# Moving the 64 sums over ada_w out of the first block, into the feed-forward part and the start of the second block

## The chip, the cores and the metric

One core of one Trainium2 chip runs the whole program. The metric is the device time of one execution in microseconds (us), the median of the runs. Times inside an execution come from one profiled execution, and are counted from the start of its span.

## What is computed

Two transformer blocks run one after the other on 256 tokens of width 1024 (T = 256, D = 1024). The second one is modulated: six vectors of 1024 numbers, computed from a conditioning vector `c` and the matrix `ada_w`, shift, scale and gate it, and two more (from `c_ctx`) shift and scale its context.

```python
def first_block(x, ...):
    proj = rmsnorm(x) @ w_in                  # latents, differential q/k/v, 2048 gate columns
    # latent attention (8 heads) and differential attention (4 heads x 2), causal
    x = x + (g_mla * (o_mla @ w_branch_mla) + g_diff * (o_diff @ w_branch_diff)) @ w_out
    x = x + (silu(hn @ w_ffn_gate) * (hn @ w_ffn_up)) @ w_ffn_down     # hn = rmsnorm(x), hidden width 2816
    return rmsnorm(x, norm_final_g)

def second_block(x, c, ctx, c_ctx, ada_w, ada_b, ...):
    mod_x = silu(c) @ ada_w + ada_b           # ada_w is 1024 x 6144
    mod_c = silu(c_ctx) @ ada_w + ada_b
    sh1, sc1, g1, sh2, sc2, g2 = split(mod_x); csh1, csc1 = first two parts of mod_c
    hx = rmsnorm(x) * (1 + sc1) + sh1; hc = rmsnorm(ctx) * (1 + csc1) + csh1
    zx = hx @ w_in2; zc_kv = hc @ w_in2[:, 1024:]
    # pooling and neighbourhood attention on zx, zc_kv
    x = x + g1 * (mixed @ w_out2)
    h2 = rmsnorm(x) * (1 + sc2) + sh2
    x = x + g2 * peer(h2)                     # 8 heads, 16 experts each out of 16384
    return rmsnorm(x, final_g)
```

## The kernel before

The program is written out by hand for each engine (`tensor_program`, `scalar_program`, `vector_program`, `pool_program`, `sync_program`); each engine runs its own list in the order written, and semaphores tie the lists together. So the order of code in a function is the order on its engine.

**The ring.** All weights come through five slots (`RING_SLOTS`), in the order of `ring_plan`. A block is 512 KB, 128 rows of 1024 words. SP issues its load when the slot is released, that is when TensorE is done with the block five places earlier. ScalarE (ACT) copies it to a rounded high part (`sb_hi`, line 922), and VectorE (DVE, line 1244) or GpSimd (POOL, line 1812) subtracts that from the raw words to give the low part (`sb_lo`). The rule that shares them out is `POOL_SHARE`: in the feed-forward part every second block is POOL's, in the context panels of the second block all of them. TensorE multiplies with the high part first, then with the low part. `hi_until` and `lo_until` run three blocks ahead of the panel that an engine serves (`AHEAD`).

**The stages.** First block: input panels (`lat`, `d`), `uq`, `ukv`, gate panels, causal attention (softmax on DVE and ACT, 32 items, with gate panels between them), branch panels `b_mla`, `b_diff`, and `w_out`. GpSimd also does the rotary embedding (`rope`, lines 1832 to 1838), in small operations. Then the feed-forward part: 11 units `u`, each with a gate panel, an up panel and the rows of `w_down` (`rows_onto`). With unit 8 the context tokens come through a ring slot, and are normalised. The second block starts with the context panels `ctx_in2` 2 and 3, beside which the last norm of the first block ("mid") runs, then the norm "mix", the panels `in2` 1, 2, 3, and the neighbourhood attention with panel `in2` 0 beside it.

**The sums over ada_w.** The vectors are computed transposed: row block m of `ada_w.T` (128 x 1024, 512 KB) times the broadcast row silu(c) or silu(c_ctx), summed along the row, gives eight columns per vector. Each is one operation on DVE (line 1260, output `sb_ada_junk`, the sum goes into a column). There are 48 row blocks, and 64 sums, since the first 16 blocks are needed for c and c_ctx. They are issued by `take_ada(key)`, whose number per place is the table `ADA_POINTS`; `ada_slot` gives each block its buffer, and `ada_loads` the place in the ring's order behind which SP issues its load, where it first waits for the sum that used the buffer before. `mod_columns` adds the bias and, for g1 and g2, makes the diagonal that `gate_row` turns into a row by two matmuls. ACT takes silu of `c_rows` (128 x 2048 words) once, at line 991.

**Around the norm "mix".** DVE's order there is: the scaling of "mid" (line 1580), the copy of the first context panel, low parts, the copy of the second, then `norm_both("mix")` with the sum of squares (line 1285) and the scaled rows (line 1523), on which TensorE's transposes for the norm wait (line 570).

## Time and profile before

| what | value |
|---|---|
| median of 3 runs | 1603.01 us (1602.9 to 1603.34) |
| profiled execution | 1604.01 us, of it 1602.2 us of span |
| mean granted TensorE clock | 0.953 of full |
| busy: PE, PEld, DVE, ACT, POOL | 1429.9, 1287.4, 939.9, 711.7, 564.4 us |
| first block up to w_out | about 0 to 270 us |
| feed-forward part | about 272 to 471 us |
| context panels, norm "mix" | about 471 to 508 us |
| in2 panels, neighbourhood attention | about 508 to 608 us |

A busy share over the whole span says little, since the stages have different limits. The clock is given as a share of full speed; 1.00 is 2.4 GHz, and 0.50 the lower level of 1.2 GHz. An engine's idle time counts only where the next thing that ends last is behind it.

### The profile page before, as it was taken

Reading aid. Unit: us, or ns where it says so; the run is one execution under the profiler, and the core shown is the slowest. Engines: PE = TensorE matmul, PEld = TensorE weight load, DVE = VectorE, ACT = ScalarE, POOL = GpSimd, SP = SyncE. Lnnn points to the kernel's source line nnn. Section 1 sums busy time; section 2 is a strip of 40 time slices with the busy share of each in tenths; the row PEclk is TensorE's granted clock in tenths of the full one; section 3 lists DMA queues with packets and bytes.
Section 4 is the critical chain, followed back from the end, with each engine's and each line's share of the span. In section 5 each row is a group of like instructions: output and inputs, shape, how many; then the busy total and the mean of one; then the engine's idle time right before and its main releaser. Section 6 shows DMA issues by size and latency. Waiting matters only on the chain.

```text
span 1602.2 us, 21914 instructions
## 1 busy us (share of the span) xinstructions
PE 1429.9 (89%) x8932; PEld 1287.4 (80%) x8932; DVE 939.9 (59%) x1493; ACT 711.7 (44%) x991; POOL 564.4 (35%) x314
## 2 busy tenths in 40 slices
PE   6878878999997987977467799999999999999997
PEld 6767767999886766877466688999999999999996
DVE  4786677544455565799788655544444444444444
ACT  4544444544444454432222344544444444444442
POOL 2661012444354103677588721221212222121222
PEclk9999879999999999989788899999999999999999
DMA  8564335777774614534200066666555655555554
GB/s 269 157 187 128 110 116 189 250 234 247 238 242 135 204 59 134 173 95 142 82 1 1 21 201 196 209 190 191 185 188 190 188 186 188 191 185 188 191 187 171
DMA packets 183124, 265.74 MB, mean 166 GB/s; under 512 B 8384, under 2 KB 119744, under 8 KB 182768
## 3 DMA queue, kind: packets, MB, share of 16 engines
q1 hardware_dynamic: 182048, 261.47, 50.8%
q8 instruction: 71, 1.16, 0.3%
q0 software_dynamic: 400, 1.25, 0.3%
q10 hardware_dynamic: 576, 1.63, 0.3%
q14 instruction: 29, 0.24, 0.0%
HBM read 259.85 MB, written 4.46 MB: 165 GB/s over the span
## 4 chain that ended last, share of the span: by engine, by line
PE 70%; DVE 14%; POOL 7%; issue 3%; DMA 3%; ACT 2%; SPq 0%; DVEq 0%; POOLq 0%; ACTq 0%
PE bank L614 21%; PE bank L645 17%; PE bank L619 10%; PE bank L650 8%; POOL sb_hot L1951 5%; PE bank L587 4%; PE bank L591 2%; DVE sb_ada_junk L1260 2%; DMA sb_raw<-w_in 2%; PE bank L890 2%; DVE sb_hot L1761 1%; DVE sb_lo L1244 1%; PE bank L829 1%; PE bank L732 1%; PE bank L848 1%
## 5 line engine op out<-in xcount | busy, mean ns | idle before, releaser
L1812 POOL TENSOR_TENSOR sb_lo<-sb_raw,sb_hi 128x1024 fp32r<-128x1024 f32 (+1 forms) x152 | 373.9, 2467 | 904.3 <-ACT sb_hi L922 904.3
L922 ACT ACTIVATE sb_hi<-sb_raw 128x1024 fp32r<-128x1024 f32 (+2 forms) x427 | 444.5, 1048 | 402.0 <-DMA sb_raw<-peer_v 128.7
L1244 DVE TENSOR_TENSOR sb_lo<-sb_raw,sb_hi 128x1024 fp32r<-128x1024 f32 (+2 forms) x276 | 361.7, 1316 | 412.4 <-ACT sb_hi L922 411.8
L614 PE MATMUL bank<-sb_act_hi,sb_hi 128*128 128x256 f32 x1632 | 410.0, 288 | 5.2 <-ACT sb_hi L922 5.2
L614 PE MATMUL bank<-sb_act_lo,sb_hi 128*128 128x256 f32 x1632 | 407.1, 286 | 0.0
L614 PEld LDWEIGHTS bank<-sb_act_hi,sb_hi 128*128 128x128 f32 x1632 | 318.2, 195 | 9.1 <-issue 4.8
L614 PEld LDWEIGHTS bank<-sb_act_lo,sb_hi 128*128 128x128 f32 x1632 | 318.5, 195 | 2.7 <-issue 0.2
L619 PE MATMUL bank<-sb_act_hi,sb_lo 128*128 128x256 f32 x1632 | 233.0, 286 | 21.0 <-POOL sb_lo L1812 21.0
L645 PE MATMUL bank<-sb_hi,sb_hid_lo 128*128 128x512 f32 x600 | 234.3, 391 | 0.0
L645 PE MATMUL bank<-sb_hi,sb_hid_hi 128*128 128x512 f32 x600 | 234.1, 390 | 0.0
L619 PEld LDWEIGHTS bank<-sb_act_hi,sb_lo 128*128 128x128 f32 x1632 | 213.9, 195 | 22.4 <-POOL sb_lo L1812 22.4
L650 PE MATMUL bank<-sb_lo,sb_hid_hi 128*128 128x512 f32 x600 | 160.4, 389 | 0.0
L650 PEld LDWEIGHTS bank<-sb_lo,sb_hid_hi 128*128 128x128 f32 x600 | 112.6, 188 | 23.4
L645 PEld LDWEIGHTS bank<-sb_hi,sb_hid_lo 128*128 128x128 f32 x600 | 112.9, 188 | 21.8
L645 PEld LDWEIGHTS bank<-sb_hi,sb_hid_hi 128*128 128x128 f32 x600 | 112.9, 188 | 21.4
L890 PE MATMUL bank<-sb_hot 128*128 128x128 f32 x512 | 88.0, 332 | 44.3 <-POOL sb_hot L1951 43.6
L890 PEld LDWEIGHTS bank<-sb_hot 128*128 128x128 f32 x512 | 78.2, 236 | 54.3 <-issue 54.2
L1951 POOL TENSOR_TENSOR sb_hot<-sb_hot,sb_pick_T 128x512 f32<-128x512 f32 x64 | 114.4, 1817 | 20.9 <-DVE sb_hot L1761 20.9
L1761 DVE TENSOR_TENSOR sb_hot<-sb_const,sb_pick_T 128x1024 f32<-128x1024 f32 x64 | 107.8, 1708 | 20.1 <-PE bank L890 19.7
L1260 DVE CUSTOM_DVE_ANT_0 sb_ada_junk<-sb_ada_w,sb_c_rows 128x1024 bf16<-128x1024 f32 x64 | 84.2, 1338 | 2.9 <-ACT sb_c_rows L991 2.9
L962 ACT ACTIVATE sb_G<-bank 128x512 f32<-128x512 f32 x64 | 38.2, 597 | 100.2 <-PE bank L890 100.2
L1536 DVE TENSOR_TENSOR sb_hid_lo<-sb_hid,sb_hid_hi 128x512 fp32r<-128x512 f32 x75 | 51.9, 692 | 52.4 <-ACT sb_hid_hi L1212 44.7
(317 smaller groups left out, 1467.6 us busy)
## 6 DMA issues: line engine op xcount, KB each, us to landing
sb_raw<-peer_uT SPq DMA_DIRECT2D x128, 512.0 KB, 3.7
sb_raw<-peer_v SPq DMA_DIRECT2D x128, 512.0 KB, 3.6
sb_raw<-w_in SPq DMA_DIRECT2D x52, 512.0 KB, 4.4
sb_ada_w<-ada_wT SPq DMA_DIRECT2D x48, 512.0 KB, 5.0
sb_raw<-w_gate SPq DMA_DIRECT2D x22, 512.0 KB, 3.9
sb_raw<-w_up SPq DMA_DIRECT2D x22, 512.0 KB, 4.1
sb_raw<-w_down SPq DMA_DIRECT2D x22, 512.0 KB, 3.9
sb_raw<-w_out SPq DMA_DIRECT2D x16, 512.0 KB, 4.4
```

What stands on the lines that cost most here:

```text
L587: e.matmul(opened[t][:, 0:n], part[:, k0 + k, t * P:(t + 1) * P], hi[:, k, :], start=i == first_i and k == 0 and part is x.hi, stop=False)
L614: e.matmul(bank[:, j * T:(j + 1) * T], hi[:, k, j * P:(j + 1) * P], part[:, k0 + k, :], start=i == first_i and j == 0 and k == 0 and part ...
L619: ins = e.matmul(bank[:, j * T:(j + 1) * T], lo[:, k, j * P:(j + 1) * P], x.hi[:, k0 + k, :], start=False, stop=i == last_i and j == 1 and ...
L645: e.matmul(psum(acc, 2 * half_ + t)[:, :], part[:, k, t * P:(t + 1) * P], hi[:, k, :], start=first and k == 0 and part is hid.hi, stop=False)
L650: ins = e.matmul(psum(acc, 2 * half_ + t)[:, :], hid.hi[:, k, t * P:(t + 1) * P], lo[:, k, :], start=False, stop=last and k == 1)
L890: ins = e.matmul(bank[:, j * P:(j + 1) * P], hot[q % HID_BUFS][:, 1, j, :], hot[q % HID_BUFS][:, 0, j, :], start=True, stop=True)
L922: e.activation(flat_of(i, "hi"), flat_of(i, "raw"), ACT.Copy).then_inc(hi_done[i % R], 1)
L1244: e.tensor_tensor(flat_of(i, "lo"), flat_of(i, "raw"), flat_of(i, "hi").bitcast(F32), ALU.subtract).then_inc(lo_done[i % R], 1)
L1260: e.tensor_tensor_reduce(ada_junk[n % 2], ada_bufs[b], c_rows[:, row], 1.0, 0.0, ALU.mult, ALU.add, mcol[name][:, c:c + 1]).then_inc(*ada_ ...
L1761: e.tensor_tensor(hot[q % HID_BUFS], iota.unsqueeze(1).unsqueeze(1).to_broadcast([P, 2, TG, P]), pT[:, 0:2, toks].unsqueeze(3).to_broadcas ...
L1812: e.tensor_tensor(flat_of(i, "lo"), flat_of(i, "raw"), flat_of(i, "hi").bitcast(F32), ALU.subtract).then_inc(lo_done[i % R], 1)
L1951: e.tensor_tensor(h, h, pT[:, 2, q * TG:(q + 1) * TG].unsqueeze(2).to_broadcast([P, TG, P]), ALU.mult).then_inc(*hot_done.inc(q))
```

## The change

The 40 sums that stood in the first block go. The feed-forward part takes 43 (before 16): one behind each gate panel's low parts, two behind each unit's hidden product, one behind each pair of `w_down` blocks. The second block takes 21 (before 8): four behind each of the two context panels' copies, four behind `in2` 1 and 2, three behind `in2` 3, two behind `in2` 0. The silu of `c_rows` moves on ACT from the front of the first block to behind the norm of the feed-forward part. The columns and rows made of the sums move later too: csh1 and csc1 to unit 8, sh1 and sc1 to unit 9, g1's diagonal to unit 10 and its two matmuls behind `in2` 1, sh2 and sc2 behind `in2` 3. Buffers: four for the first 28 row blocks, then seven.

```diff
-ADA_FIRST_BUFS, ADA_BUFS = 3, 4
+ADA_FFN_BUFS, ADA_BUFS = 4, 7
...
-N_ADA, N_ADA_FIRST = 6 * DC, 3 * DC
+N_ADA, N_ADA_FFN = 6 * DC, 28
...
-ADA_POINTS = ([(("lat", 1), 1), (("d", 0), 1), (("d", 1), 2), (("d", 2), 2)]
...
+ADA_POINTS = ([(("w_gate", 0), 1), (("w_up", 0), 1)] + [p for u in range(1, N_FFN) for p in ((("w_gate", u), 1), (("w_up", u), 2), (("down", u - 1), 1))]
+              + [(("down", N_FFN - 1), 1)]
+              + [(("ctx_in2", j), 4) for j in (2, 3)] + [(("in2", j), 4) for j in (1, 2)] + [(("in2", 3), 3), (("in2", 0), 2)])
...
-                after = 6 + m if m < N_ADA_FIRST else span["w_out", 1][-1] + 6 + 2 * (m - N_ADA_FIRST)
+                after = span["down", N_FFN - 1][-1] + 6 + m - N_ADA_FFN
...
@@ scalar_program
-            act.wait_ge(c_in, 32)
-            e.activation(c_rows, c_rows, ACT.Silu).then_inc(*silu_c.inc())
...
             norm_out("ffn", col("norm_ffn_g", 0, 8))
-            act.wait_ge(*ada_done.at(*ada_last[N_ADA_FIRST - 1]))
+            act.wait_ge(c_in, 32)
+            e.activation(c_rows, c_rows, ACT.Silu).then_inc(*silu_c.inc())
...
@@ vector_program
-            ffn_mods = {0: ("csh1", "csc1"), 1: ("sh1", "sc1"), 2: ("g1",), 10: ("sh2", "sc2")}
+            ffn_mods = {8: ("csh1", "csc1"), 9: ("sh1", "sc1"), 10: ("g1",)}
...
                     hid_left(("ffn", u), i)
+                    take_ada("w_up", u)
+                    for name in ffn_mods.get(u, ()):
+                        mod_columns(name)
...
             ctx_copy(2)
+            take_ada("ctx_in2", 2)
             lo_until(("ctx_in2", 3))
             ctx_copy(3)
+            take_ada("ctx_in2", 3)
             norm_both("mix", xr, [normed.at("mid", 1)], [])
```

Three places show what moves. In the names, `sb_ada_junk` is a sum's throwaway output, the row of `sb_mod` alone is the write of its result, and the number behind a name tells buffers apart.

DVE, before, between the copies of the second `uq` panel and of the second `ukv` panel in the first block:

```order
L1319 COPY sb_qm_89<-bank6 128x384
L1260 ISA sb_ada_junk1_118,sb_mod_128<-sb_ada_w1_111,sb_c_rows_108 128x1024
L1260 ISA sb_mod_128 128x1
L1260 ISA sb_ada_junk0_117,sb_mod_128<-sb_ada_w1_111,sb_c_rows_108 128x1024
L1260 ISA sb_mod_128 128x1
L1319 COPY sb_kv_91<-bank0 128x512
L1260 ISA sb_ada_junk1_118,sb_mod_128<-sb_ada_w2_112,sb_c_rows_108 128x1024
L1260 ISA sb_mod_128 128x1
L1260 ISA sb_ada_junk0_117,sb_mod_128<-sb_ada_w2_112,sb_c_rows_108 128x1024
L1260 ISA sb_mod_128 128x1
L1244 TENSOR_TENSOR sb_lo3_63<-sb_raw3_62,sb_hi3_64 128x1024
L1319 COPY sb_kv_91<-bank2 128x512
```

The same place in the changed program:

```order
L1320 COPY sb_qm_89<-bank6 128x384
L1320 COPY sb_kv_91<-bank0 128x512
L1245 TENSOR_TENSOR sb_lo3_63<-sb_raw3_62,sb_hi3_64 128x1024
L1320 COPY sb_kv_91<-bank2 128x512
L1414 COPY sb_km_90<-sb_kv_91 128x8x64 x2
```

The copies and the low parts follow each other with no sum between them; it is so at all 40 places of the first block.

DVE, changed, from the second context panel's low parts to the sum of squares of the norm "mix" (line 1286):

```order
L1245 TENSOR_TENSOR sb_lo1_55<-sb_raw1_54,sb_hi1_56 128x1024
L1320 COPY sb_zc_134<-bank5 128x512
L1261 ISA sb_ada_junk0_117,sb_mod_128<-sb_ada_w0_110,sb_c_rows_108 128x1024
L1261 ISA sb_mod_128 128x1
L1261 ISA sb_ada_junk1_118,sb_mod_128<-sb_ada_w1_111,sb_c_rows_108 128x1024
L1261 ISA sb_mod_128 128x1
L1261 ISA sb_ada_junk0_117,sb_mod_128<-sb_ada_w2_112,sb_c_rows_108 128x1024
L1261 ISA sb_mod_128 128x1
L1261 ISA sb_ada_junk1_118,sb_mod_128<-sb_ada_w3_113,sb_c_rows_108 128x1024
L1261 ISA sb_mod_128 128x1
L1286 ISA sb_xs_76,sb_stat_71<-sb_xres_73 128x1024
```

Before, the sum of squares stands directly behind the copy of `sb_zc`; now four sums stand between them. Four more stand behind the other copy of `sb_zc`, ahead of three low parts.

SP, changed, its queue of loads across the end of the feed-forward part (`w_in2` blocks are the context panels'):

```order
L1975 DMA sb_raw2_58<-w_in2 128x2x512
L1982 DMA sb_ada_w3_113<-ada_wT 128x1024
L1982 DMA sb_ada_w0_110<-ada_wT 128x1024
L1988 DMA sb_band_135<-band 128x2048
L1990 DMA sb_pool_w_136<-pool_w 128x512
L1975 DMA sb_slot3_61<-norm_final_g 128x1024
L1975 DMA sb_raw4_66<-w_in2 128x2x512
L1982 DMA sb_ada_w1_111<-ada_wT 128x1024
L1975 DMA sb_raw0_50<-w_in2 128x2x512
L1982 DMA sb_ada_w4_114<-ada_wT 128x1024
L1975 DMA sb_raw1_54<-w_in2 128x2x512
```

Before, this piece has no load of `ada_wT` at all: the last of the feed-forward part stands ahead of the last `w_down` block, and the next one comes in the middle of the `in2` panels.

## Rows read from the trace of the kernel before

**Rows 1.** The page: costliest groups, and DMA issues, of the sums.
```profile
L1260 DVE CUSTOM_DVE_ANT_0 sb_ada_junk<-sb_ada_w,sb_c_rows 128x1024 bf16<-128x1024 f32 x64 | 84.2, 1338 | 2.9 <-ACT sb_c_rows L991 2.9
...
sb_ada_w<-ada_wT SPq DMA_DIRECT2D x48, 512.0 KB, 5.0
```

**Rows 2.** Windows by stage: length, busy time of each engine, clock, DMA share, GB/s.
```profile
60.00:120.00 60.00, 48.58 (x298) 43.86 (x297) 51.89 (x67) 25.63 (x37) 39.99 (x42) 0.94 0.64 194
120.00:208.00 88.00, 78.06 (x489) 67.64 (x488) 57.08 (x159) 42.73 (x127) 7.13 (x3) 0.86 0.35 108
208.00:275.00 67.00, 50.26 (x301) 45.40 (x300) 50.17 (x83) 30.53 (x48) 14.11 (x7) 0.90 0.54 181
```

**Rows 3.** Windows of the sums alone: DVE busy, count, clock, DMA share, GB/s.
```profile
36.00:283.00 247.00, 53.16 (x40) 0.90 0.48 151
283.00:480.00 197.00, 19.44 (x16) 0.99 0.74 241
```

**Rows 4.** Waits of PE, 40 to 285 us: in total, times, longest.
```profile
PE bank L614 <- DVE sb_ob_lo L1328: 9.3, 1, 9.3
PE bank L587 <- ACT sb_hi L922: 8.6, 2, 7.0
PE bank L591 <- POOL sb_lo L1812: 6.7, 1, 6.7
PE bank L732 <- DVE sb_prob_T L1319: 6.0, 6, 2.8
...
PE bank L719 <- ACT sb_score_bufs L1037: 3.7, 2, 1.9
PE bank L619 <- POOL sb_lo L1812: 3.2, 1, 3.2
```

**Rows 5.** Timeline of ACT at the silu of c_rows: start, us, instruction.
```profile
41.30 1.28 ACT L991 ACT_TABLE_LOAD   x1
42.59 1.91 ACT L991 ACTIVATE sb_c_rows<-sb_c_rows 128x2048 f32<-128x2048 f32 x1
```

**Rows 6.** Timelines of DVE and POOL in the rotary embedding of qm.
```profile
88.62 1.48 DVE L1260 CUSTOM_DVE_ANT_0 sb_ada_junk<-sb_ada_w,sb_c_rows 128x1024 bf16<-128x1024 f32 x1
...
88.97 1.44 POOL L1833 TENSOR_TENSOR sb_rope_tmp<-sb_qm,sb_rope 128x128 f32<-128x128 f32 x1
90.37 0.46 POOL L1834 TENSOR_TENSOR sb_rope_tmp<-sb_qm,sb_rope 128x128 f32<-128x128 f32 x1
```

**Rows 7.** Windows of line 614 alone, at the b_diff panels: PE, PEld, clock, DMA.
```profile
229.00:234.00 5.00, 3.76 (x16) 3.49 (x16) 0.50 0.01 3
235.00:240.00 5.00, 3.48 (x28) 3.22 (x27) 1.00 0.84 279
```

**Rows 8.** Six units of the feed-forward part: window; DVE's and POOL's low parts.
```profile
301.50:403.40 101.90, 101.90 (x718) 95.48 (x717) 50.18 (x62) 43.41 (x47) 44.22 (x18) 1.00 0.74 237
...
L1244 DVE TENSOR_TENSOR sb_lo<-sb_raw,sb_hi 128x1024 fp32r<-128x1024 f32 x18 | 25.5, 1417 | 48.6 <-ACT sb_hi L922 48.6
...
L1812 POOL TENSOR_TENSOR sb_lo<-sb_raw,sb_hi 128x1024 fp32r<-128x1024 f32 x18 | 44.4, 2469 | 59.0 <-ACT sb_hi L922 59.0
```

**Rows 9.** Timelines at the norm "mix": DVE, then PE.
```profile
496.46 3.93 DVE L1244 TENSOR_TENSOR sb_lo<-sb_raw,sb_hi 128x1024 fp32r<-128x1024 f32 x3 [7.07 <-ACT sb_hi L922]
500.91 1.22 DVE L1285 CUSTOM_DVE_ANT_0 sb_xs<-sb_xres 128x1024 f32<-128x1024 f32 x1
...
504.11 2.15 PE L570 MATMUL bank<-sb_const,sb_xs 128*128 128x128 f32 x9 [5.84 <-DVE sb_xs L1523]
```

**Rows 10.** Chain that ended last, at the context panels: start, us, what.
```profile
471.67 5.97 DMA sb_raw<-w_in
...
478.80 4.78 POOL sb_lo L1812 x2
484.19 4.62 DVE sb_xres L1580 x2
```

**Rows 11.** DMA, 466 to 480 us in 40 slices: rate of the queues.
```profile
GB/s 345 222 64 76 12 187 257 222 281 322 316 380 380 415 392 404 363 410 380 433 392 410 416 386 410 392 299 263 228 146 222 217 193 234 222 252 181 170 252 146
```

More of the change, by code:

```diff
@@ L393, in build @@
         c_in = sem("c_in")
-        ada_in = [sem(f"ada{i}_in") for i in range(ADA_FIRST_BUFS + ADA_BUFS)]
+        ada_in = [sem(f"ada{i}_in") for i in range(ADA_BUFS)]
         early_stored = [sem(f"early{i}_stored") for i in range(3)]
@@ L467, in build @@
                 after = ada_block[ada_last[before]] + 7
+            elif m < N_ADA_FFN:
+                after = span["w_out", 1][-1] + 6 + 2 * m
             else:
-                after = 6 + m if m < N_ADA_FIRST else span["w_out", 1][-1] + 6 + 2 * (m - N_ADA_FIRST)
+                after = span["down", N_FFN - 1][-1] + 6 + m - N_ADA_FFN
             ada_loads.setdefault(after, []).append(m)
@@ L789, in tensor_program @@
                 whole(steps)
+                if j == 1:
+                    gate_row("g1")
                 if j == 2:
@@ L1488, in vector_program @@
                 e.tensor_tensor(merged[:, 2 * j:2 * j + 2, :], by_chunk(psum(("b_mla", j))[:, :]), gates_T[:, 2 * j:2 * j + 2, :], ALU.mult).then_inc(*gives(("b_mla", j)))
-                take_ada("b_mla", j)
             for i0 in (0, 2):
@@ L1509, in vector_program @@
                     e.tensor_tensor(v, psum(("w_out", j), t)[:, :], v, ALU.add).then_inc(*gives(("w_out", j), t))
-                if j == 0:
-                    take_ada("w_out", j)
             def norm_both(stage, src, ready, xs_free):
@@ L1609, in vector_program @@
                     heads_out("q", q_T, 4)
+            for name in ("sh2", "sc2"):
+                mod_columns(name)
             def beside_na():
@@ L1984, in load_until @@
                             sp.wait_ge(*ada_done.at(*ada_last[before]))
-                        elif m >= N_ADA_FIRST:
-                            sp.wait_ge(*full(("w_out", 1), NT - 1))
+                        else:
+                            sp.wait_ge(*(full(("w_out", 1), NT - 1) if m < N_ADA_FFN else full("ffn_acc", 3)))
                         e.dma_start(ada_bufs[slot], a["ada_wT"][m * P:(m + 1) * P, :]).then_inc(ada_in[slot], 16)
```

32 lines of the change are left out of this document (9 added, 23 removed).

## The prediction

> **What bounds the kernel now.** I read the page's groups first, for what the sums cost as work: 64 on DVE, 84 us in all, and 48 loads of 512 KB [rows 1]. Then windows by stage and windows of the sums alone: 40 of the 64 stand before 283 us, in 53 us of DVE time, and 16 in the feed-forward part [rows 3]. Then I asked in each stage what TensorE (PE) waits for, since PE has by far the most work; a microsecond of a sum counts only where PE waits behind it.
>
> In the first block PE does wait. From 60 to 275 us DVE is busy 159 of 215 us, and from 60 to 120 us it is the fullest engine, 51.9 of 60 [rows 2]. Six kinds of wait between 40 and 285 us come to 37.5 us [rows 4]; the norm's own wait before the feed-forward part is left out, since the change doesn't touch it. In the feed-forward part PE is busy 101.9 of 101.9 us over six units, while DVE stood idle 48.6 us waiting for ACT's high parts, and POOL 59.0 [rows 8]. So the sums leave a stage where their engine is late and go mostly to one where it has time. The exception is the norm "mix": there PE waits 5.84 us for DVE [rows 9], and the change puts sums directly in front of it.
>
> **The first block, what is taken away.** Durations are of one execution, whose own time was 1604.0 us, 1.0 above the median; I make the sum on that and take 1.0 off at the end.
>
> *Silu on ACT.* The table load and the silu, 1.28 and 1.91 us [rows 5], are directly in front of the high parts for which PE waits 7.0 us [rows 4]. Gain 3.2 us (bounds 2 and 3.2). At its new place ACT loads the silu table anyway for the first hidden unit, and before it waited at that place for the last of the 40 sums; so I cost it at nothing there, behind the three blocks that PE has ready. If that cover were gone it would be 1.9 us, once.
>
> *POOL's rotary embedding.* An operation of POOL that takes 0.46 us alone takes 1.44 when it starts beside a sum of DVE [rows 6]. I count eleven of the 36 such operations between 68 and 99 us lengthened by a sum (the two kinds that differ are shown), 0.7 to 1.0 us each, about 10 us with one low part of POOL. This chain ends in POOL's low parts, for which PE waits 6.7 and 3.2 us [rows 4]. The first wait closes; of the second about 1.1 us stays, because PE arrives earlier too. Gain 8.8 (bounds 5, if other work of DVE stretches them instead, and 9.9, both waits whole).
>
> A page bears on it. The Trainium skill, "SBUF — State Buffer", says that DVE and GpSimd share one port pair as an exclusive lock, and that a DVE operation with two SBUF inputs and a GpSimd one that reads SBUF cannot run together. The 0.46 against 1.44 us agree with it. By the lock alone the gain here would be the whole blocked time, 11 x 1.0 = 11 us, an estimate from that page; I take the smaller number since only PE's waits can be given back.
>
> *Causal attention.* The waits for `sb_prob_T` and for `sb_score_bufs`, 6.0 and 3.7 us [rows 4], follow on pairs of sums, each about 2.4 us (19.44 / 16 = 1.2 us a sum [rows 3]), that stand ahead of the next scores and copies. Gain 7.5 of 9.7 (bounds 4 and 9.7); the rest is the latency of the softmax chain.
>
> *Branch panels.* PE waits 9.3 us for `sb_ob_lo` [rows 4], and in DVE's order four sums and the four products of b_mla stand ahead of it. Four sums are 4.8 us; one low part that POOL blocked may come free as well. Gain 5.5 (bounds 4.5 and 7.3). The second wait for high parts, 8.6 - 7.0 = 1.6 us [rows 4], is at w_out's last block behind DVE's chain of merges with three sums in it: gain 1.6 (bounds 0 and 1.6).
>
> *The clock.* After the 9.3 us wait the granted clock is 0.50, and 16 matmuls of a panel take 3.76 us where 28 take 3.48 at full clock [rows 7]: 0.235 against 0.124 us each. Over the three stages the clock takes (1 - 0.94) x 60 + (1 - 0.86) x 88 + (1 - 0.90) x 67 = 22.6 us [rows 2], partly idle time. With the waits closed, fewer stretches fall to 0.50. Which ones, no row can say; I take 6 us (bounds 1 and 16).
>
> Sum of gains: 3.2 + 8.8 + 7.5 + 5.5 + 1.6 + 6.0 = 32.6 us.
>
> **The later places, what is added.** *Feed-forward part.* 27 more sums at 1.2 us are 32 us of DVE time in 205. Per unit they add two, 2.4 us, where DVE idles 48.6 / 6 = 8.1 us [rows 8]; cost nothing while that cover holds. The loads stay two a unit up to unit 7, since two sums share a block, and become four from unit 8. At unit 9 the extra sums, sh1 and sc1 stand ahead of the context norm's low parts; ACT waits for those inside its own list, and the high parts queued behind it come 2.4 to 3 us later against a lead of about three blocks. I take 1.0 (bounds 0 and 3). g1's two matmuls only change place, about 1.7 us on PE in both.
>
> *The norm "mix".* DVE's chain there: low parts until 500.3, copy, sum of squares at 500.91, and PE's transposes at 504.11 after 5.84 us of waiting [rows 9]. The first four sums fit into the 7.07 us in which DVE waited for high parts [rows 9]. The second four stand between the copy and the sum of squares: 4 x 1.2 less the overlap of back-to-back sums, 4.6 us, entirely on the path (bounds 4.6 and 7, with one of them blocked by a POOL low part). Queued behind them are the norm, PE's transposes and all `in2` panels.
>
> *Their loads.* Two blocks of `ada_wT` now stand ahead of the band, the gain row and the load issued at 471.67, and one behind it. That load took 5.97 us, and ACT, two POOL low parts and the "mid" scaling hang on it in a row [rows 10]. The queues run at about 400 GB/s between 470 and 475 us [rows 11], so a load of 512 KB takes 1.3 us of them and two take 2.6. I take 2.7, with a little of the third (bounds 0, if the queue has drained, and 5).
>
> *in2 panels and the second attention.* Each of the panels `in2` 1 to 3 is preceded or followed by a burst of up to four loads, and up to three more sums; PE was never idle there, a burst of four takes 4 x 1.3 = 5.2 us of the queues, which is about two blocks of the three that lie ready: 1.0 (bounds 0 and 4). One sum fewer in `in2` 0 (-1.2) and a later start of the attention (+1.5): 0.3.
>
> Sum of costs: 1.0 + 4.6 + 2.7 + 1.0 + 0.3 = 9.6 us. Nothing behind 608 us changes.
>
> 1604.0 - 32.6 + 9.6 = 1581.0, less 1.0 for the median: **1580.0 us**.
>
> **The rivals.** *A, the sum above* (chance 0.63): between 1570 and 1591.
>
> *B, half of the gain is lost in the first block* (0.19): closing one wait uncovers the next, above all the ring's loads, whose slots are released by PE itself, or the softmax chain. For it: the DMA share of 0.64 from 60 to 120 us [rows 2]; against it: the 24 row blocks that the sums load there, 12.6 MB, leave that stage too. Gain 17, costs 9.6: 1603 - 17 + 9.6 = 1595.6; up to 1600.
>
> *C, more* (0.12): the clock stays at its upper level almost through, 16 instead of 6, and the costs at the mix norm stay at the low bound: 1603 - 42.6 + 6.5 = 1567.
>
> *D, slower: DVE and POOL block each other in the feed-forward part* (0.06). Six units take 101.9 us; POOL's low parts take 44.4 and DVE's 25.5 of them [rows 8], twelve sums 14.6 and twelve more as much again: 99 us of work that cannot overlap, if DVE and POOL exclude each other there as in [rows 6]. If low parts come late by 3 us a unit, PE loses 33 us over 11 units: 1603 - 32.6 + 9.6 + 33 = 1613. It decides from about 2.1 us a unit (23 / 11). Against it: low parts run three blocks ahead, and a block of PE takes 101.9 / 36 = 2.8 us, so 8.5 us. A POOL low part of 2.47 us [rows 8] can hold a sum up, and a sum a low part. The Trainium skill, "SBUF — State Buffer", has it so: of two operations that need the shared pair, the second waits for the whole of the first.
>
> **How the numbers follow.** A measurement tells this kernel's change from none at about 0.2%, 3.2 us. Range: A, and somewhat over half of B and of C, 0.81 together: 1568 to 1597. Faster by over 0.2%: A, B and C, 0.94; within 0.2%: 0.02; slower: 0.04; these two are D.
>
> **What would show it.** Right: no sums before 270 us; POOL's rotary operations at 0.3 to 0.5 us; the first block ends about 33 us earlier; PE still full in the feed-forward part; the wait before the mix norm 12 to 14 us instead of 5.84, with four sums in front of the sum of squares. Wrong: waits for low parts of PE in the feed-forward units (D), waits for high parts behind DMA in the first block (B), or a wait at unit 8's context block much over its 2.9 us.

## The result, and the profile after

The changed kernel takes **1582.49 us** (median of 4 runs, 1576.31 to 1585.24) against 1602.97 us (4 runs); the ratio is 0.9866, with a 95% interval of 0.9837 to 0.9896. It is faster by 20.5 us. The forecast was 1580.0 (1568 to 1597).

The profiled execution of it took 1583.26 us, with a span of 1581.4. I laid TensorE's landmarks of both traces side by side: the first transposes of a norm (rows of line 570 before, 572 after), and the first matmul of the first context panel.

| landmark on PE | before | after | lead |
|---|---|---|---|
| end of the attention stage, ahead of the first `b_mla` panel | 215.35 | 190.15 | 25.2 |
| norm ahead of the feed-forward part | 272.00 | 239.87 | 32.1 |
| first context panel | 471.48 | 438.78 | 32.7 |
| norm "mix" | 504.11 | 482.31 | 21.8 |
| norm behind the second attention | 638.07 | 617.95 | 20.1 |
| end of the span | 1602.2 | 1581.4 | 20.8 |

So all of the gain arises before 240 us, the feed-forward part keeps it, and a third of it is lost in one stretch of 44 us, between the first context panel and the norm "mix".

**The first block.** The waits of PE after, 40 to 285 us (in total, times, longest); they answer to [rows 4]:

```profile
PE bank L621 <- POOL sb_lo L1807: 6.1, 1, 6.1
PE bank L572 <- DVE sb_xs L1514: 5.3, 1, 5.3
PE bank L616 <- DVE sb_ob_lo L1329: 3.6, 1, 3.6
PE bank L589 <- ACT sb_hi L924: 3.0, 1, 3.0
PE bank L734 <- DVE sb_prob_T L1320: 2.8, 6, 0.8
PE bank L616 <- ACT sb_hi L924: 0.7, 1, 0.7
PE bank L721 <- ACT sb_score_bufs L1037: 0.2, 1, 0.2
```

The six kinds of [rows 4] were 37.5 us; their successors here (without L572, the norm's own) are 16.4. The wait for POOL's first low part (6.7) is gone, but the second has grown from 3.2 to 6.1. That is 21.1 us of the 32.1 in the table of landmarks; most of the rest is the clock. The whole attention stage, from the end of POOL's second wait to the first `b_mla` panel, in windows (length, PE, PEld, DVE, ACT, POOL busy, clock, DMA share, GB/s), before and then after:

```profile
102.24:215.35 113.11, 101.64 (x680) 90.52 (x680) 78.11 (x203) 58.97 (x157) 14.02 (x7) 0.89 0.37 117
```

```profile
93.39:190.15 96.76, 93.47 (x680) 84.26 (x680) 56.17 (x168) 57.95 (x156) 11.79 (x7) 0.97 0.32 93
```

Both hold the same 680 matmuls. The stage is 16.35 us shorter: 8.2 us less idle time (113.11 - 101.64 against 96.76 - 93.47), and 8.2 us less busy time for the same matmuls. Where the latter comes from is seen in windows of 4 us of PE alone, in the trace of before (length, PE busy, clock, DMA share, GB/s):

```profile
124.00:128.00 4.00, 1.13 (x9) 1.00 0.84 262
128.00:132.00 4.00, 4.00 (x24) 0.57 0.00 0
132.00:136.00 4.00, 3.48 (x27) 1.00 0.51 135
...
164.00:168.00 4.00, 1.97 (x8) 0.72 0.73 262
168.00:172.00 4.00, 4.00 (x21) 0.50 0.00 0
172.00:176.00 4.00, 4.00 (x23) 0.93 0.38 131
```

Up to 127.45 PE waited 2.81 us for `sb_prob_T`, and up to 166.79 it waited 2.03. Behind each wait stands a stretch at or near the lower level, 1.2 GHz, in which PE is full and does 21 to 24 matmuls in 4 us; from 136 to 144 us, at 1.00, it does 35. Two more waits of the stage, of 1.94 us (up to 152.11) and 1.73 us (up to 194.31), are followed by windows at 0.57 and 0.56. So these four waits cost about as much again behind them. After the change the longest wait in the stage is 0.81 us, and from 100 to 190 us the granted clock is 1.00 throughout.

**The sums at their new places** (the page's group, and its DMA issue), against [rows 1]:

```profile
L1261 DVE CUSTOM_DVE_ANT_0 sb_ada_junk<-sb_ada_w,sb_c_rows 128x1024 bf16<-128x1024 f32 x64 | 119.2, 1894 | 1.2 <-DMA sb_ada_w<-ada_wT 1.2
...
sb_ada_w<-ada_wT SPq DMA_DIRECT2D x48, 512.0 KB, 5.9
```

The same 64 sums take 119 us instead of 84. They stand beside POOL's low parts now, and each side holds the other up. This is the window of [rows 8] moved by the lead of 32.1 us, so over the same six units, with POOL's low parts in it:

```profile
269.40:371.30 101.90, 101.90 (x722) 96.15 (x721) 83.16 (x78) 44.83 (x48) 51.70 (x18) 1.00 0.77 249
...
L1807 POOL TENSOR_TENSOR sb_lo<-sb_raw,sb_hi 128x1024 fp32r<-128x1024 f32 x18 | 51.7, 2872 | 51.7 <-ACT sb_hi L924 51.7
```

POOL's low parts rose from 2469 to 2872 ns and DVE's busy time from 50.2 to 83.2 us, and PE is still busy 101.90 of 101.90 us. The whole part took 198.9 us (239.87 to 438.78), before 199.5.

**The stretch that lost.** It is 43.5 us long, before 32.6. DVE's timeline (start, us) at the end of the feed-forward part, where PE's last product ended at 438.95:

```profile
437.55 2.36 DVE L1267 TENSOR_TENSOR sb_stat<-sb_stat,sb_cols 128x8 f32<-128x8 f32 x1
439.94 5.91 DVE L1276 TENSOR_SCALAR sb_gate_diag<-sb_const,sb_stat 128x128 f32<-128x128 f32 x8
445.76 1.22 DVE L1261 CUSTOM_DVE_ANT_0 sb_ada_junk<-sb_ada_w,sb_c_rows 128x1024 bf16<-128x1024 f32 x1
...
446.90 1.22 DVE L1261 CUSTOM_DVE_ANT_0 sb_ada_junk<-sb_ada_w,sb_c_rows 128x1024 bf16<-128x1024 f32 x1
...
448.05 2.48 DVE L1555 TENSOR_TENSOR sb_xres<-bank,sb_xres 128x512 f32<-128x512 f32 x4
```

The four adds of `ffn_acc` onto `sb_xres` (the last row) end 11.6 us after PE's last product; before they ended 0.9 us after it. In front of them stand sums, g1's bias and its diagonal. Those that ran beside POOL's low parts were slowed: a sum at 434.19 took 3.42 us, the bias (128x8) 2.36 us, the eight tiles of the diagonal 5.91 us. POOL was idle from 444.6 to 448.3, and the two sums there took 1.22 us each, as when alone. SP's queue of loads shows a second effect:

```profile
439.46 0.51 SPq L1975 DMA_DIRECT2D sb_raw<-w_in  x1
447.01 0.33 SPq L1982 DMA_DIRECT2D sb_ada_w<-ada_wT  x1
447.38 0.43 SPq L1975 DMA_DIRECT2D sb_raw<-w_in  x1
```

SP stood still for 7 us, because the load of `ada_wT` at 447.01 needs a buffer that the delayed sum at 445.76 was using; the load of `w_in2` queued behind it came as late. It had stood still once before, until 437.65, behind the sum that took 3.42 us, so that the band (1 MB) and the gain row went out just ahead of the `w_in2` load of 439.46. ACT's squares of "mid" stand in its list behind the high parts of those blocks:

```profile
452.89 1.06 ACT L924 ACTIVATE sb_hi<-sb_raw 128x1024 fp32r<-128x1024 f32 x1 [4.64 <-DMA sb_raw<-w_in]
453.85 1.04 ACT L1106 ACTIVATE sb_xs<-sb_xres 128x1024 f32<-128x1024 f32 x1
```

The squares started 14.9 us after PE's last product (before 8.5). They did not wait for the adds, which had ended 3.3 us earlier, but for the high part ahead of them, and this for its load. "mid" scaled its rows 18.1 us after the product (before 12.6). Last, PE at the mix norm, against the row of PE in [rows 9]:

```profile
482.31 3.00 PE L572 MATMUL bank<-sb_const,sb_xs 128*128 128x128 f32 x13 [10.43 <-DVE sb_xs L1514]
```

I split the 10.9 us that the stretch lost at the start of "mid"'s scaling: 5.5 us (18.1 - 12.6) ahead of it, and 5.4 (25.3 - 19.9) behind it, where the second four sums stand. Below, "the product" is PE's last product of the feed-forward part.

### The profile page after: what moved, and what is told of

It reads as the page before. It is cut to its first block, busy times and chain, and to the rows that moved or that the text cites. A ratio compares the mean times of both kernels' runs of the same rounds, so it can differ in the third digit from the quotient of the medians.

```text
span 1581.4 us, 21911 instructions
## 1 busy us (share of the span) xinstructions
PE 1426.2 (90%) x8932; PEld 1284.4 (81%) x8932; DVE 974.3 (62%) x1493; ACT 708.7 (45%) x989; POOL 560.5 (35%) x314
## 4 chain that ended last, share of the span: by engine, by line
PE 53%; DVE 10%; POOL 5%; DMA 1%; issue 1%; ACT 1%; SPq 0%; DVEq 0%; ACTq 0%
PE bank L647 15%; PE bank L616 14%; PE bank L652 7%; PE bank L621 7%; POOL sb_hot L1946 5%; PE bank L589 3%; PE bank L892 2%; DVE sb_hot L1756 2%; PE bank L593 1%; PE bank L831 1%; PE bank L850 1%; DVE sb_i12f L1695 1%; DMA sb_raw<-w_in 1%; DVE sb_pick L1716 1%; DVE sb_eq L1707 1%
## 5 line engine op out<-in xcount | busy, mean ns | idle before, releaser
L1807 POOL TENSOR_TENSOR sb_lo<-sb_raw,sb_hi 128x1024 fp32r<-128x1024 f32 (+1 forms) x152 | 382.8, 2525 | 879.1 <-ACT sb_hi L924 879.0
L621 PE MATMUL bank<-sb_act_hi,sb_lo 128*128 128x256 f32 x1632 | 232.6, 286 | 23.2 <-POOL sb_lo L1807 23.2
L647 PEld LDWEIGHTS bank<-sb_hi,sb_hid_lo 128*128 128x128 f32 x600 | 112.9, 188 | 21.8
L1261 DVE CUSTOM_DVE_ANT_0 sb_ada_junk<-sb_ada_w,sb_c_rows 128x1024 bf16<-128x1024 f32 x64 | 119.2, 1894 | 1.2 <-DMA sb_ada_w<-ada_wT 1.2
```

Of the source, the lines that this page charges most:

```text
L621: ins = e.matmul(bank[:, j * T:(j + 1) * T], lo[:, k, j * P:(j + 1) * P], x.hi[:, k0 + k, :], start=False, stop=i == last_i and j == 1 and ...
L647: e.matmul(psum(acc, 2 * half_ + t)[:, :], part[:, k, t * P:(t + 1) * P], hi[:, k, :], start=first and k == 0 and part is hid.hi, stop=False)
L1261: e.tensor_tensor_reduce(ada_junk[n % 2], ada_bufs[b], c_rows[:, row], 1.0, 0.0, ALU.mult, ALU.add, mcol[name][:, c:c + 1]).then_inc(*ada_ ...
L1807: e.tensor_tensor(flat_of(i, "lo"), flat_of(i, "raw"), flat_of(i, "hi").bitcast(F32), ALU.subtract).then_inc(lo_done[i % R], 1)
```

## The experiments

Each was timed in rounds with the kernel before on the same chip; its median there was 1602.0 to 1604.0 us. "Stretch" is from PE's first context matmul to the mix norm.

### What the sums of the first block cost, each stage by itself

Three kernels are the one before with some sums over 8 words instead of 1024, the place, the load and the silu being kept.

```diff
-                    e.tensor_tensor_reduce(ada_junk[n % 2], ada_bufs[b], c_rows[:, row], 1.0, 0.0, ALU.mult, ALU.add,
+                    wd = 8 if key[0] in ("lat", "d", "uq", "ukv", "gate", "b_mla", "b_diff", "w_out") else D
+                    e.tensor_tensor_reduce(ada_junk[n % 2][:, 0:wd], ada_bufs[b][:, 0:wd], c_rows[:, row][:, 0:wd], 1.0, 0.0, ALU.mult, ALU.add,
```

> The kernel before, with the 40 sums of the first block over 8 words instead of 1024, so that csh1, csc1, sh1, sc1 and g1 are not the reference's; the loads, the silu and all places stay. This is the removal alone, without the later costs. By the prediction's terms it gains 8.8 (rotary embedding) + 7.5 (attention) + 5.5 + 1.6 (branch panels) + 6 (clock) = 29.4 us: 1573.5, and the feed-forward part's norm starts at 242.6 instead of 272.0. Rival (the 24 loads of the first block, 12.6 MB, hold up the ring's loads as well): 24 us or less, 1579 or more. If the changed kernel's 32.1 us there are 3 to 4.4 for the silu, 28 to 29 are left for this kernel and none for the loads.

Measured 1574.58 us (1571.41 to 1576.91), ratio 0.9826 (0.9811 to 0.9842): 28 us. The feed-forward part's norm starts at 244.80, 27.2 us earlier than before, against the 28 to 29 that the changed kernel gained there without the silu. The rival falls: with all 24 loads still there the gain is over its 24 us, and what the loads held up is 1 to 2 us at most.

The second has only the 16 sums beside the attention short:

```diff
+                    wd = 8 if key[0] == "gate" else D
```

> The kernel before, with the 16 sums behind its eight gate panels, that is beside the attention, over 8 words instead of 1024; parts of sh1, sc1 and g1 are not the reference's. From the end of the second wait for POOL's low parts to the first b_mla panel the kernel before takes 113.1 us, the changed one 96.8; the waits for the softmax there sum to 9.1 and 2.3 us, and the clock of 120 to 208 us was 0.86. Theory 1 (the waits pull the clock down, and the clock costs more than they do): the whole 14 to 16 us come back from these 16 sums alone, time 1587 to 1589, clock about 1.00 there. Theory 2 (the clock has another cause, for instance the stage ahead): 7 us, 1596.

Measured 1588.09 us (1583.92 to 1588.29), ratio 0.9897 (0.988 to 0.9913): 16 us, from 16 sums.

```profile
103.28:198.09 94.81, 91.35 (x680) 82.04 (x680) 63.38 (x206) 59.20 (x157) 13.22 (x7) 1.00 0.46 145
```

This is the window of the attention stage again: the same 680 matmuls in 91.35 us, at clock 1.00. The idle time in it fell by 8.0 us (11.5 to 3.5) and the busy time by 10.3. No sum ahead of the stage was changed, so theory 1 stands: with the waits gone, the clock stays up.

The third has only the 14 sums from `lat` to `ukv` short:

```diff
+                    wd = 8 if key[0] in ("lat", "d", "uq", "ukv") else D
```

> The kernel before, with the 14 sums from the latent panel to the second ukv panel over 8 words instead of 1024; parts of csh1, csc1, sh1 and sc1 are not the reference's. The prediction gave 8.8 us to them by POOL's rotary operations. Theory 1 (as predicted): the waits of TensorE for POOL's low parts go from 6.7 and 3.2 to 0 and 1.1, time 1594. Theory 2 (other work of VectorE, low parts and copies, blocks POOL in place of the sums, and TensorE arrives earlier): the first wait goes, the second becomes 5 to 6 us, gain 4 to 5, time 1598 to 1599.

Measured 1596.61 us (1594.57 to 1600.25), ratio 0.9961 (0.9946 to 0.9975): 6 to 7 us. PE's waits for POOL there, in one row where before there were two of 6.7 and 3.2:

```profile
PE bank L619 <- POOL sb_lo L1813: 5.1, 1, 5.1
```

The waits are theory 2's; the time lies between the two. In the trace the feed-forward norm starts 6.0 us earlier, 4.8 of them in these waits. Why the second wait stays is seen in POOL's timeline of the changed kernel, and DVE's beside it:

```profile
82.33 0.47 POOL L1827 TENSOR_TENSOR sb_rope_tmp<-sb_qm,sb_rope 128x128 f32<-128x128 f32 x1 [7.68 <-DVE sb_qm L1320]
...
83.59 1.45 POOL L1830 TENSOR_TENSOR sb_rope_tmp<-sb_qm,sb_rope 128x128 f32<-128x128 f32 x1
...
86.76 1.44 POOL L1828 TENSOR_TENSOR sb_rope_tmp<-sb_qm,sb_rope 128x128 f32<-128x128 f32 x1
88.16 1.52 POOL L1829 TENSOR_TENSOR sb_rope_tmp<-sb_qm,sb_rope 128x128 f32<-128x128 f32 x1
...
91.00 2.34 POOL L1807 TENSOR_TENSOR sb_lo<-sb_raw,sb_hi 128x1024 fp32r<-128x1024 f32 x1
```

```profile
83.39 1.32 DVE L1245 TENSOR_TENSOR sb_lo<-sb_raw,sb_hi 128x1024 fp32r<-128x1024 f32 x1 [0.72 <-ACT sb_hi L924]
...
86.40 1.48 DVE L1245 TENSOR_TENSOR sb_lo<-sb_raw,sb_hi 128x1024 fp32r<-128x1024 f32 x1
88.14 1.23 DVE L1245 TENSOR_TENSOR sb_lo<-sb_raw,sb_hi 128x1024 fp32r<-128x1024 f32 x1 [0.26 <-ACT sb_hi L924]
```

POOL had idled 7.7 us: the chain can't start before DVE has copied `sb_qm` out of the banks. Then three operations of 0.46 us still take 1.45, now beside DVE's own low parts at 83.39, 86.40 and 88.14. So a chain of 8.7 us with a low part of 2.3 behind it stays, and PE waits for its end.

### The silu alone, put back

The changed kernel, with ACT's silu at its old place:

```diff
@@ scalar_program
+            act.wait_ge(c_in, 32)
+            e.activation(c_rows, c_rows, ACT.Silu).then_inc(*silu_c.inc())
             for j, dst in enumerate((dq, dk, dv)):
...
             norm_out("ffn", col("norm_ffn_g", 0, 8))
-            act.wait_ge(c_in, 32)
-            e.activation(c_rows, c_rows, ACT.Silu).then_inc(*silu_c.inc())
```

> The changed kernel, with the silu of c_rows back at its old place on ScalarE, in front of the high parts of the first panels. Theory 1 (the silu and its table load, 1.28 + 1.91 us, were on the path): TensorE's wait at 40 us grows from 2.98 to about 6.2 and the time by 3.2 to 1585.7. Theory 2 (the loads bound that stage, and the silu sat in a wait for them): time stays within 1 us of 1582.5.

Measured 1586.88 us (1583.61 to 1587.44), ratio 0.9903 (0.9885 to 0.9921); PE's wait at 40 us:

```profile
PE bank L589 <- ACT sb_hi L924: 6.0, 1, 6.0
```

It grew from 2.98 to 5.99, 3.0 us, as theory 1 has it. The medians differ by 4.4; the 1.4 more are within the scatter of the runs. The intervals of the two ratios overlap (0.9885 to 0.9921, and 0.9837 to 0.9896), so the wait in the trace decides.

### The four sums ahead of the mix norm

```diff
-            take_ada("ctx_in2", 3)
             norm_both("mix", xr, [normed.at("mid", 1)], [])
             norm_lo("mix")
+            take_ada("ctx_in2", 3)
```

> The changed kernel, with the four sums between the copy of the second context panel and the norm "mix" moved behind that norm's low parts. Theory 1 (the four sums are wholly on the path, as the prediction has it): the wait of TensorE before the mix norm falls from 10.43 us by 4.6 to about 5.8, and the time from 1582.5 to about 1578. Theory 2 (that wait comes from late loads and from the chain ahead of the second context panel, and the sums only fill it): the wait stays over 9 us and the time stays at 1582. Theory 3: the four sums only move, and now hold up the copies and low parts for the panel in2 1; a new wait of 2 to 5 us there, time 1580 to 1583.

Measured 1578.04 us (1574.86 to 1581.31), ratio 0.9852 (0.9832 to 0.9872).

```profile
476.67 1.73 PE L572 MATMUL bank<-sb_const,sb_xs 128*128 128x128 f32 x7 [5.82 <-DVE sb_xs L1514]
```

The wait is 5.82 us, before the change 5.84, and the median is 4.4 us lower: theory 1. The intervals of the ratios overlap (0.9832 to 0.9872, and 0.9837 to 0.9896), so here too the 4.6 us are read from the wait and not from the times. There was no new wait in the panel `in2` 1, so theory 3 falls. The stretch is still 38.8 us against 32.6.

### What makes "mid" late: the diagonal, the loads, or the sums

One kernel moves g1's bias and diagonal behind the mix norm:

```diff
-            ffn_mods = {8: ("csh1", "csc1"), 9: ("sh1", "sc1"), 10: ("g1",)}
+            ffn_mods = {8: ("csh1", "csc1"), 9: ("sh1", "sc1")}
...
             norm_lo("mix")
+            mod_columns("g1")
```

> The changed kernel, with g1's bias and its diagonal of eight tiles moved on VectorE from the end of the feed-forward part (unit 10) to behind the low parts of the norm "mix". In the changed kernel they take 2.36 and 5.91 us from 437.55 us on, and behind them stand two sums, the adds of ffn_acc at 448.05 and the sum for whose end SyncE's queue of loads waits until 447.01. Theory 1 (this lateness is what the end of the feed-forward part lost beyond the forecast): the adds come 6 to 8 us earlier, the w_in2 load issued at 447.38 comes at about 441, the small waits of TensorE in the context panels (6.1 us in all) fall to about 3, and the time is 1578 to 1580. Theory 2 (the amount of the loads there, 512 KB each at 1.3 us of the queues, is what counts): the adds come earlier but TensorE's waits stay, time 1582.

Measured 1582.42 us (1580.44 to 1583.17), ratio 0.9875 (0.9856 to 0.9894): no gain, against theory 1's 3 us. With the diagonal away, the sums behind it run beside POOL's low parts:

```profile
436.26 3.42 DVE L1261 CUSTOM_DVE_ANT_0 sb_ada_junk<-sb_ada_w,sb_c_rows 128x1024 bf16<-128x1024 f32 x1
...
439.62 3.42 DVE L1261 CUSTOM_DVE_ANT_0 sb_ada_junk<-sb_ada_w,sb_c_rows 128x1024 bf16<-128x1024 f32 x1
...
442.96 3.41 DVE L1261 CUSTOM_DVE_ANT_0 sb_ada_junk<-sb_ada_w,sb_c_rows 128x1024 bf16<-128x1024 f32 x1
...
446.30 2.48 DVE L1555 TENSOR_TENSOR sb_xres<-bank,sb_xres 128x512 f32<-128x512 f32 x4
```

The adds still end 7.8 us after PE's last product. SP no longer stood still there (the next `w_in2` load at 443.76, 2.8 us after the product instead of 8.4), but the one before it, issued at 441.57 with the others in flight, was used by ACT only at 450.36, 8.8 us later; in the changed kernel this took 7.7 us, and before the change 6.0. "mid" started 16.1 us after the product. So with the standstill gone the loads in flight took over: the time is theory 2's.

Both moves in one kernel:

> Both of the two moves above, the four sums and g1's diagonal behind the norm "mix". If each is on the path by itself the gains add up to 7 to 9 us: 1574 to 1576. If they share one wait (the norm's start is set by whichever is later) the time is that of the better one, 1578. VectorE then has 4.6 + 5 us of work ahead of the copies of the panel in2 1, and if low parts become late there, up to 5 us come back.

Measured 1576.92 us (1574.52 to 1578.13), ratio 0.9843 (0.9826 to 0.986), 1.1 less than with the four sums alone, which these runs can't tell from nothing; stretch 38.0. ACT's wait for the `w_in2` load that was issued at 438.30, 9.5 us before its use:

```profile
447.84 1.06 ACT L924 ACTIVATE sb_hi<-sb_raw 128x1024 fp32r<-128x1024 f32 x1 [9.27 <-DMA sb_raw<-w_in]
```

SP issued its next `w_in2` load at 440.25, without a standstill, the adds ended 7.8 us after the product, and "mid" started only 17.2 us after it.

The next takes volume off the queues and leaves DVE alone:

```diff
-                        e.dma_start(ada_bufs[slot], a["ada_wT"][m * P:(m + 1) * P, :]).then_inc(ada_in[slot], 16)
+                        wd = 8 if m in (24, 25, 26, 27, 31, 32, 33, 34) else D
+                        e.dma_start(ada_bufs[slot][:, 0:wd], a["ada_wT"][m * P:(m + 1) * P, 0:wd]).then_inc(ada_in[slot], 16)
```

> The changed kernel, with eight of the loads of ada_wT around the end of the feed-forward part (row blocks 24 to 27 and 31 to 34) cut from 1024 to 8 words per row; all sums keep their full length, over what the buffers held, so g1 and parts of sh2 and sc2 are not the reference's. This takes 4 MB off the queues between about 405 and 452 us and nothing off VectorE. Theory 1 (volume: the w_in2 load issued at 439.46 landed 7.7 us later because two loads of ada_wT, the band and the gain row were ahead of it): it lands within 6 us, the stretch from the first context panel to the mix norm shrinks from 43.5 us by 2 to 4, time 1578.5 to 1580.5. Theory 2 (only VectorE's work ahead of the norm counts): stretch and time unchanged, 1582.

Measured 1581.0 us (1576.73 to 1581.92), ratio 0.9863 (0.9845 to 0.9882); stretch 43.0, adds 11.6 us and "mid" 17.5 us after the product. The `w_in2` load issued at 437.07 was used 7.2 us later instead of 7.7, and not within the 6 of theory 1. Taking these eight loads away alone gives 0.6 us of the stretch. But SP still stood still for the sum, until 444.62, so this kernel does not show what the transfers cost once nothing else holds "mid" up.

The opposite leaves the loads and takes DVE's time of the 21 sums of the second block away:

```diff
+                    wd = 8 if key[0] in ("ctx_in2", "in2") else D
```

> The changed kernel, with its 21 sums of the second block over 8 words instead of 1024, so that g2 and parts of sh2 and sc2 are not the reference's; all loads stay. This takes VectorE's time of these sums away and leaves their loads. Theory 1 (the second four sums are the only ones on the path): as the kernel with these four moved, 4.6 us, time 1578; the stretch from the first context panel to the mix norm stays about 6 us longer than before (32.6), from the loads. Theory 2 (the first four, 6.2 us with one lengthened, delay the low parts and the second copy too): stretch within 2 us of before, time 1572 to 1574.

Measured 1577.46 us (1576.91 to 1579.65), ratio 0.985 (0.9836 to 0.9863); stretch 39.6, "mid" 19.0 us after the product and the mix norm 20.5 behind that. Theory 1: beyond the second four, no cost of the second block's sums is seen; what is left is ahead of "mid".

### Versions that take both away

The first attempt was crude: five sums a unit, none beside the context panels.

```diff
-ADA_POINTS = ([(("w_gate", 0), 1), (("w_up", 0), 1)] + [p for u in range(1, N_FFN) for p in ((("w_gate", u), 1), (("w_up", u), 2), (("down", u - 1), 1))]
+ADA_POINTS = ([(("w_gate", 0), 1), (("w_up", 0), 1)] + [p for u in range(1, N_FFN) for p in ((("w_gate", u), 1), (("w_up", u), 2), (("down", u - 1), 2))]
               + [(("down", N_FFN - 1), 1)]
-              + [(("ctx_in2", j), 4) for j in (2, 3)] + [(("in2", j), 4) for j in (1, 2)] + [(("in2", 3), 3), (("in2", 0), 2)])
+              + [(("in2", 1), 4), (("in2", 2), 3), (("in2", 3), 2), (("in2", 0), 2)])
```

> Five sums a unit in the feed-forward part instead of four (two behind each pair of w_down blocks), none beside the context panels, four, three, two and two in the in2 panels; g1's diagonal behind the norm "mix"; the loads for the second block issued some blocks later than in the changed kernel. 53 sums stand in the feed-forward part. If the cover there holds (TensorE still full, 199 to 200 us for the part) and both VectorE's sums and the loads beside the context panels were what the stretch to the mix norm lost, that stretch is back to 33 to 35 us and the time is 1571 to 1574. If only the four sums on the path counted: 1576 to 1578. Against it: 0.9 loads more per unit, and a fifth sum beside POOL's low parts; if low parts come late by 1 us a unit the time is 1582 or more.

Measured 1586.03 us (1585.6 to 1586.4), ratio 0.9899 (0.9884 to 0.9915): slower than the change. The feed-forward part takes 206.0 us instead of 198.9; PE waits twice 0.5 us for DVE's low parts in the middle of it, and between 395 and 431 us 1.6, 4.0 and 1.5 us for high parts (before the change two such waits stood in the part, of 0.9 and 2.9 us; what delays them more here was not taken apart). And four slowed sums now stand ahead of the adds, which end 11.1 us after the product. So at four sums a unit the cover of the feed-forward part holds. At five it starts to give: 1.0 us of waits for low parts is seen, and whether the late high parts belong to it is open.

This kernel also parts the adds from the loads. Its adds end about as late as the changed kernel's, but SP's four `w_in2` loads behind the product have no load of `ada_wT` between them and no standstill. "mid" starts 15.3 us after the product, not 18.1, and here ACT does wait for an add:

```profile
457.16 1.06 ACT L1108 ACTIVATE sb_xs<-sb_xres 128x1024 f32<-128x1024 f32 x1 [1.18 <-DVE sb_xres L1557]
```

The second attempt clears DVE's way to the adds: no sums in unit 10 behind its gate panel, five a unit only up to unit 5, 20 in the second block.

```diff
+ADA_POINTS = ([(("w_gate", 0), 1), (("w_up", 0), 1)] + [p for u in range(1, N_FFN - 1) for p in ((("w_gate", u), 1), (("w_up", u), 2), (("down", u - 1), 2 if u <= 5 else 1))]
+              + [(("w_gate", N_FFN - 1), 1)]
+              + [(("ctx_in2", j), 3) for j in (2, 3)] + [(("in2", j), 4) for j in (1, 2, 3)] + [(("in2", 0), 2)])
...
+            norm_both("mix", xr, [normed.at("mid", 1)], [])
+            norm_lo("mix")
+            mod_columns("g1")
+            take_ada("ctx_in2", 3)
...
+            if m >= N_ADA_FFN:
+                after = max(after, span["down", N_FFN - 1][-1] + 8 + m - N_ADA_FFN)
```

> The changed kernel, with nothing ahead of the adds of ffn_acc on VectorE at the end of the feed-forward part: the four sums of unit 10 behind its gate panel go, five instead of four a unit stand in units 1 to 5, three sums behind the first context copy, three and g1's diagonal behind the norm "mix", four each behind in2 1 to 3, two behind in2 0; loads for the second block later. In the changed kernel the adds end 11.6 us after TensorE's last product of the part, before 0.9; the scaling of "mid" starts 18.1 us after it, before 12.6. Theory 1 (this lateness is 5.5 of the 10.9 us that the stretch to the mix norm lost, and the second four sums the rest): adds end at about 1, "mid" starts at 12.5 to 13.5, the mix norm 33 to 34 us after the last product instead of 43.4, time 1572 to 1574. Theory 2 (the loads of w_in2 themselves are slowed by the other loads in flight): "mid" starts at 15 or later, time 1575 to 1577.

Measured 1576.5 us (1569.71 to 1578.16), ratio 0.9823 (0.9802 to 0.9843). The feed-forward part takes 201.2 us, with two waits of 0.5 us for DVE's low parts again, so the fifth sum isn't quite free in units 1 to 5 either. The adds end 0.9 us after PE's last product and "mid" starts 10.7 us after it, earlier than before the change. So the first 5.5 us came from what this kernel took away there: DVE's late work, SP's standstills behind it, and the loads of `ada_wT` among the `w_in2` loads (none stands between the four of 440.13 to 448.66). It took them away together, so it does not say how much is whose, and it is no test of its theory 2, the loads in flight. With only a part of it taken away "mid" stayed late: 17.5 us after the product with the eight loads cut, 16.1 and 17.2 without the second standstill, and 15.3 in the kernel with five sums a unit, where the adds were late but not the loads. But the norm "mix" came 34.6 us after the product. ACT's timeline behind "mid":

```profile
459.67 1.06 ACT L926 ACTIVATE sb_hi<-sb_raw 128x1024 fp32r<-128x1024 f32 x1 [5.25 <-DMA sb_raw<-w_in]
463.40 1.06 ACT L926 ACTIVATE sb_hi<-sb_raw 128x1024 fp32r<-128x1024 f32 x1 [2.68 <-DMA sb_raw<-w_in]
466.00 1.06 ACT L926 ACTIVATE sb_hi<-sb_raw 128x1024 fp32r<-128x1024 f32 x1 [1.54 <-DMA sb_raw<-w_in]
468.64 1.06 ACT L926 ACTIVATE sb_hi<-sb_raw 128x1024 fp32r<-128x1024 f32 x1 [1.58 <-DMA sb_raw<-w_in]
```

The four blocks come 2.6 us apart and more: a load of `ada_wT` stands in front of each but the first. The last kernel moves these:

```diff
-                after = max(after, span["down", N_FFN - 1][-1] + 8 + m - N_ADA_FFN)
+                after = max(after, span["down", N_FFN - 1][-1] + (8 if m < N_ADA_FFN + 3 else 13 + (m - N_ADA_FFN - 3) // 2))
```

> The kernel adds_first with its loads of ada_wT for the second block moved: three behind the fourth w_in2 load (where the queues have time, before the scaling of "mid" gives the gain row's slot back), the others not before the last w_in2 block of the second context panel. In adds_first the scaling of "mid" started 10.7 us after TensorE's last product (before: 12.6), but the mix norm came 23.9 us after that start (before: 19.9), and ScalarE waited 2.68, 1.54 and 1.58 us for the three w_in2 loads that followed the first one, each with a load of ada_wT in front of it; before 0.83, 0.29, 0.30. Theory 1 (these loads in front are the 4 us): the waits fall to under 1 us each, mix norm 30 to 31.5 us after the last product instead of 34.6, time 1572 to 1573.5. Theory 2 (VectorE's three sums there, two of them lengthened by POOL, are what holds it up): it stays at 34 and the time at 1576. The burst of paired loads then falls beside in2 1 to 3, and up to 2 us may come back there.

Measured **1573.04 us** (1565.44 to 1576.06), ratio 0.9818 (0.9792 to 0.9843). ACT and PE:

```profile
461.61 1.06 ACT L926 ACTIVATE sb_hi<-sb_raw 128x1024 fp32r<-128x1024 f32 x1 [5.24 <-DMA sb_raw<-w_in]
463.58 1.06 ACT L926 ACTIVATE sb_hi<-sb_raw 128x1024 fp32r<-128x1024 f32 x1 [0.91 <-DMA sb_raw<-w_in]
464.90 1.06 ACT L926 ACTIVATE sb_hi<-sb_raw 128x1024 fp32r<-128x1024 f32 x1 [0.26 <-DMA sb_raw<-w_in]
466.26 1.06 ACT L926 ACTIVATE sb_hi<-sb_raw 128x1024 fp32r<-128x1024 f32 x1 [0.30 <-DMA sb_raw<-w_in]
```

```profile
472.30 1.94 PE L574 MATMUL bank<-sb_const,sb_xs 128*128 128x128 f32 x8 [5.03 <-DVE sb_xs L1516]
```

The last blocks come 1.3 us apart, the norm 30.6 us after the product (before the change 32.5). Theory 1. The median is 9.4 us under the changed kernel's, by the ratios 7.7 us; the intervals of the two ratios just overlap (0.9843 and 0.9837), but the step is seen in the trace.

## Why the forecast was right, point by point

The main line held: the removal gave 32.1 us up to the feed-forward part, forecast 32.6, and the costs ate about a third of it. But the parts of that sum were less good than the sum, and that it came within 0.5 us is partly luck. Ahead of the attention stage the forecast had 12.0 us (3.2 + 8.8) and 8.9 were measured; for the attention and all of the clock it had 13.5 and 16.4 were measured; for the branch panels 7.1, and 6.9. The first two errors, 3.1 too much and 2.9 too little, cancel.

- *Silu, 3.2.* Right: 3.0 us of waiting when put back alone.
- *POOL's rotary embedding, 8.8.* Over-sized. The waits went from 9.9 to 6.1 us, and 4.8 were gained with these sums alone short. The bound that I had named, "5, if other work of DVE stretches them instead", was the case. I had counted how many operations a sum lengthened, and not asked what DVE does in that time once the sums are gone: its own low parts. The trace of before shows it already, seven more of the 36 operations lengthened beside low parts of DVE; one of them:

```profile
94.69 1.47 DVE L1244 TENSOR_TENSOR sb_lo<-sb_raw,sb_hi 128x1024 fp32r<-128x1024 f32 x1
...
95.05 1.44 POOL L1834 TENSOR_TENSOR sb_rope_tmp<-sb_qm,sb_rope 128x128 f32<-128x128 f32 x1
```

The sentence of the Trainium skill, "SBUF — State Buffer", that a DVE operation with two SBUF inputs excludes a GpSimd one that reads SBUF agrees with this too, since a low part is such an operation: 1.44 to 1.52 us against 0.46 beside the low parts.
- *Attention, 7.5, and the clock, 6 over all.* Under-sized: 16.35 us in this stage alone, 8.2 in idle time and 8.2 in the same matmuls at the upper clock. I had the clock as a term by itself, spread over three stages. It belongs to each wait: the four of 1.7 to 2.8 us were each followed by a window of 4 us or more at 0.50 to 0.57 of full.
- *Branch panels, 5.5 and 1.6.* Right in sum: from the first `b_mla` panel to the feed-forward part's norm it took 56.65 us before the change and 49.72 after it, 6.9 less.
- *Feed-forward part, 1.0.* It cost nothing that the traces show (198.9 against 199.5 us; the 205 us of the forecast for the length of the part were too many). The wait at unit 8's context block was 2.4 us (before 2.9). Rival D is refuted for four sums a unit; for five PE's first waits for DVE's low parts appear.
- *The norm "mix", 4.6.* Right: 4.61 us of wait went away with the four sums (10.43 to 5.82).
- *Their loads, 2.7.* The weakest step. The place was right, the size and the reason were not. "mid" was 5.5 us late. I had charged the transfer time of two loads in the queue, and thinning the loads gave 0.6 by itself. What I had left out was DVE's work at the end of the part, a sum of 3.4 us, the bias and the diagonal, and SP, which stood behind loads that waited for one of those sums. The transfers count too, as the 8.8 and 9.5 us of a load without the second standstill show; the share of each was not measured. I had written that each load waits for the sum that used its buffer, and that sums can take longer beside POOL, and did not put the two together.
- *in2 and the attention behind it, 1.3.* Right: the lead fell by 1.7 us between the norm "mix" and the norm behind the second attention.

The wait at the mix norm was 10.43 us and not 12 to 14, since PE came to it later, by 2.8 us more of small waits in the context panels (6.4 against 3.6) and by 3.5 us more busy time for the same 98 matmuls (26.7 against 23.2) at a granted clock of 0.83 instead of 0.94. The forecast had the clock only among the gains, and not behind the waits that the change adds. The sum of it: forecast 1580.0, measured 1582.5.

Open stay what made high parts late with five sums a unit, how the 5.5 us ahead of "mid" divide between late work and transfers, and the scatter below.
